# Fifteen of sixteen hidden pairs by seven products in an MLP's down projection, and an earlier place for the join of their sums on VectorE

## What is computed

```
h = rmsnorm(x, norm_mlp)
x = x + square(relu(h @ w_up)) @ w_down      # w_up 1024 x 4096, w_down 4096 x 1024
x = rmsnorm(x, norm_final)                   # end of the first block
proj = rmsnorm_2(x, norm_mix_2) @ w_in_2     # start of the second block
```

## Time and profile before

| | us |
|---|---|
| median of 3 runs | 952.59 |
| lowest, highest | 952.55, 954.3 |
| the profiled execution | 952.69 |
| its span on the core | 950.6 |
| PE busy in it | 942.7 (99%) |
| DVE busy | 706.8 (74%) |
| ACT busy | 561.2 (59%) |
| POOL busy | 129.9 (14%) |

### The profile page before, as it was taken

One profiled execution on the slowest core, in us unless ns is written; L12 is line 12 of the kernel. 1 busy time (PEld: TensorE's weight loads), 2 busy tenths in 40 slices (PEclk: granted clock), 3 DMA queues, 4 the chain that ended last, 5 costly groups with the idle time before them and its releaser, 6 DMA issues.

```text
span 950.6 us, 17020 instructions
## 1 busy us (share of the span) xinstructions
PE 942.7 (99%) x6900; PEld 868.9 (91%) x6900; DVE 706.8 (74%) x941; ACT 561.2 (59%) x856; POOL 129.9 (14%) x181
## 2 busy tenths in 40 slices
PE   9999999999999999999999999999999999999997
PEld 7877899989999999989988999998998899999996
DVE  5767875778877887878876787776666567777777
ACT  5677554557666666656865674545455445555544
POOL 2000001005223320414000001100000012121210
PEclk9999999999999999999999999999999999999999
DMA  9974447455666666556465365555645346565661
GB/s 302 310 244 126 121 128 179 160 177 176 200 192 192 194 194 199 174 172 199 139 194 163 105 204 173 174 183 174 198 159 174 115 156 205 173 202 176 202 197 67
DMA packets 133551, 170.45 MB, mean 179 GB/s; under 512 B 5824, under 2 KB 97296, under 8 KB 133472
## 3 DMA queue, kind: packets, MB, share of 16 engines
q1 hardware_dynamic: 131408, 165.07, 56.1%
q10 hardware_dynamic: 1424, 2.84, 0.9%
q0 software_dynamic: 640, 1.44, 0.7%
HBM read 168.28 MB, written 1.05 MB: 178 GB/s over the span
## 4 chain that ended last, share of the span: by engine, by line
PE 95%; DVE 2%; DMA 1%; ACT 1%; issue 1%; SPq 0%; POOL 0%; POOLq 0%; ACTq 0%; DVEq 0%
PE ps L442 24%; PE ps L409 15%; PE ps L410 15%; PE ps L413 15%; PE ps L391 4%; PE ps L524 3%; PE ps L859 3%; PE ps L863 3%; PE ps L858 3%; PE ps L803 2%; PE ps L799 2%; PE ps L800 2%; PE ps L556 1%; PE ps L559 1%; PE ps L555 1%; DMA raws<-in_w_in 1%
## 5 line engine op out<-in xcount | busy, mean ns | idle before, releaser
L1738 DVE TENSOR_TENSOR parts<-raws,parts 128x1024 fp32r<-128x1024 f32 (+3 forms) x307 | 364.4, 1202 | 125.4 <-ACT parts L1180 124.5
L1180 ACT ACTIVATE parts<-raws 128x1024 fp32r<-128x1024 f32 (+3 forms) x307 | 309.1, 1029 | 124.8 <-PE ps L413 50.4
L409 PE MATMUL ps<-room_r,parts 128*128 128x256 f32 x1248 | 308.6, 281 | 0.0
L410 PE MATMUL ps<-room_r,parts 128*128 128x256 f32 x1248 | 306.4, 279 | 0.0
L442 PE MATMUL ps<-parts,room_r 128*128 128x512 f32 (+1 forms) x1008 | 237.7, 392 | 0.4 <-ACT parts L1180 0.4
L409 PEld LDWEIGHTS ps<-room_r,parts 128*128 128x128 f32 x1248 | 234.3, 188 | 2.2 <-issue 0.8
L410 PEld LDWEIGHTS ps<-room_r,parts 128*128 128x128 f32 x1248 | 235.0, 188 | 1.2
L442 PEld LDWEIGHTS ps<-parts,room_r 128*128 128x128 f32 x1008 | 184.2, 188 | 42.9 <-issue 1.2
L413 PE MATMUL ps<-room_r,parts 128*128 128x256 f32 x1248 | 196.6, 279 | 0.0
L413 PEld LDWEIGHTS ps<-room_r,parts 128*128 128x128 f32 x1248 | 167.7, 188 | 0.0
L1772 DVE TENSOR_TENSOR room_r<-room,room_r 128x512 fp32r<-128x512 f32 (+2 forms) x74 | 52.5, 714 | 31.3 <-ACT room_r L1469 10.1
(11 more groups left out here) (245 smaller groups left out, 1133.4 us busy)
## 6 DMA issues: line engine op xcount, KB each, us to landing
raws<-in_w_in SPq DMA_DIRECT2D x99, 512.0 KB, 4.5
raws<-in_w_ffn_in SPq DMA_DIRECT2D x44, 512.0 KB, 4.6
raws<-in_w_up SPq DMA_DIRECT2D x32, 512.0 KB, 3.9
raws<-in_w_down SPq DMA_DIRECT2D x32, 512.0 KB, 3.7
raws<-in_w_ffn_out SPq DMA_DIRECT2D x22, 512.0 KB, 4.3
raws<-in_w_xkv SPq DMA_DIRECT2D x16, 512.0 KB, 4.3
raws<-in_w_out SPq DMA_DIRECT2D x8, 512.0 KB, 4.5
raws<-in_w_up_ssd SPq DMA_DIRECT2D x8, 512.0 KB, 4.6
```

The costliest lines, as they stand in the source:

```text
L409: e.matmul(ps, wh, hT[0][:, k, :], start=k == 0, stop=False)
L410: e.matmul(ps, wh, hT[1][:, k, :], start=False, stop=False)
L1180: e.activation(t.h, t.raw, ACT.Copy).then_inc(s["hi"], 1)
L1738: e.tensor_tensor(t.l, t.raw, t.h.bitcast(F32), ALU.subtract).then_inc(s["lo"], 1)
```

## The change

`by_sums[0]` grows from 14 to 15 pairs, so that `down(14, 0)` too is made by `down_by_sums`; only pair 15 is left to the 12 plain matmuls. The join's place in DVE's list was set by `until`, from when the last seven-product pair ends; for this MLP it is now set by a tile number: the join stands right behind the rest of B13. The other MLP keeps its rule.

```diff
-        by_sums = [range(14), range(1, 10)]
+        by_sums = [range(15), range(1, 10)]
...
-        where = {}
+        where, last_rest = {}, {}
...
                     if h:
                         where["down", u, q] = Group(None, count, None)
+                        last_rest[u, q] = w_.i
...
-                until(where["product", u, 1].at)
+                if u:
+                    until(where["product", u, 1].at)
+                else:
+                    while lo <= last_rest[u, 13]:
+                        rest_of_tile()
                 e.wait_ge(s["first_product"], u + 1)
```

## The result

The changed kernel takes 959.03 us (median of 6 runs, 958.76 to 960.5), the kernel before 952.62 us (6 runs, 952.18 to 954.3). The ratio is 1.0067, 95% interval 1.0057 to 1.0077: 6.4 us slower. The forecast was 956.7 us with a range to 958.4, so the kernel became slower as forecast, and the time lies 0.6 us above the range. The profiled execution took 959.11 us, its span is 957.2 us.

What follows compares the result with a forecast made beforehand. PE, busy 942.7 of 950.6 us, was taken as the bound, so each new wait is paid in full. -0.32 + 0.1 + 3.6 + 0.7 = +4.1 us gave 956.7 us, range 955.2 to 958.4.

Steps and rivals of the forecast that it cites:

- The matmuls, -0.32 us: On PE, pair 14 goes from 12 plain matmuls (2.80 us) to 21 (2.48 us): 0.32 us less.
- Pair 14's inputs are covered: In down(14, 0), S14 and the activation sums with their rests are ready before PE wants them: no wait.
- The join at 377.6, held by ACT's copy: On DVE, the join starts at 377.6 instead of 376.46, 1.1 us later, because ACT's copy ends only at 377.55.
- 0.1 us at the eight transposes: PE reaches the eight transposes at 381.48; the second add ends about 381.9, giving a stall of 0.1 us.
- The stall of 3.6 us: Before the four transposes: B14's later rest delays C2's load, ACT waits ahead of x, PE waits 3.6 us.
- 0.7 us in C2: PE waits 0.7 us after C2's first eight matmuls, as C2's rest stands behind x times norm_final; bounds 0 and 1.
- The clock: Rival: TensorE's clock falls in the 3.6 us stall, half speed costs 2 us, time 958.7 us; chance 0.06.

Runs made afterwards that it cites:

- the run with x ahead of C2: The changed kernel with ACT's rounding of the transposed x ahead of C1 and C2; 953.92 us, ratio 1.0013 to the kernel before.
- the run of 14 pairs reordered: Kernel before, with the join behind B13's rest and ACT's join copy, x's rounding and C2's rest on DVE moved earlier; 952.49 us, ratio 0.9999.

## Why the prediction was wrong, point by point

- **The matmuls, -0.32 us:** right. PE reaches the eight transposes when the sum says, once the start's 0.5 us are taken off.
- **Pair 14's inputs are covered:** right. The waits of PE name no product of pair 14.
- **The join at 377.6, held by ACT's copy:** right, 378.31 - 0.5 = 377.8, and DVE's idle time ahead of it (0.65 us) is ended by the copy.
- **0.1 us at the eight transposes:** too small. From their start to the next matmul it is 1.07 us (382.02 to 383.09), where it was 0.80 us (381.80 to 382.60); the second add ends only at 381.21 + 1.41 = 382.62. In the run with x ahead of C2 they take as long. The term is 0.3 us.
- **The stall of 3.6 us:** right in its chain and its size. PE is idle for 3.43 us; from the start of the last two matmuls ahead of it to the transposes it is 4.06 us (388.30 to 392.36) instead of 0.47 us (387.80 to 388.27 before), 3.6 us more. C2's load was forecast at 383.1 (383.78 - 0.5 = 383.3) and 3.7 us long (ACT starts 3.82 us behind it, 383.78 to 387.60), x at 387.9 (388.56 - 0.5 = 388.1), the end of the wait at 391.7 (392.36 - 0.5 = 391.9). The chain was cut at two places, the load's lateness and the order on ACT, and each cut took about 5 us away.
- **0.7 us in C2:** right. From 401.34 the next start should be 401.46 and is 402.15, 0.69 us.
- **The clock: the step that failed.** The sum put the fall of TensorE's clock at nothing; it stood among the rivals only, with the time 958.7 (959.03 measured), the price 2 us (1.67 measured) and a chance of 0.06, and the upper end of the range, 958.4, left it out. The chance came from the earlier trace rows, where the clock held for over 4 us of rest, so that a wait of 3.6 us seemed to fall short. That reading was wrong: those rows show **when** the clock changed in one execution, not how much rest it takes. Here the level changed about 4 us behind the last full matmul too (388.9 to 392.8), but a rest of 3.4 us was enough, and PE was already at work when the price came due. Nor is "over 4 us" steady: at the end of the program, where nothing of this was changed, the clock falls between 2.1 us (the run of 14 pairs reordered) and 5.2 us (the run with 5 matmuls of the identity) behind the last matmul. The windows of both, in this order:

```profile
944.00:945.00 1.00, 0.17 (x2) 0.00 (x0) 1.00 (x3) 0.61 (x1) 0.01 (x1) 1.00 0.00 0
...
946.00:947.00 1.00, 0.00 (x0) 0.00 (x0) 0.43 (x2) 0.38 (x1) 0.53 (x1) 0.62 0.89 344
```

```profile
948.00:949.00 1.00, 0.53 (x5) 0.32 (x3) 0.74 (x2) 0.72 (x1) 0.38 (x2) 1.00 0.00 0
...
953.00:954.00 1.00, 0.00 (x0) 0.00 (x0) 0.00 (x0) 0.00 (x0) 0.00 (x0) 0.85 0.94 365
```

A mean of 0.62 in the microsecond of 946 is a fall at 946.24, with the last matmul done at 944.17; 0.85 in that of 953 is a fall at 953.70, with the last done at 948.53. One row of an end could not say that 3.6 us was too short. "TensorE: Matmul & The Clock Gate", section "HAM oscillation — how this bites in real kernels" of the Trainium skill, describes this effect of a wait on a load: the work behind it starts at the lower clock. The trace agrees, with 3.43 us idle and 0.50 granted from 392.8 us on.

The sum with the measured terms is -0.3 + 0.3 + 3.6 + 0.7 + 1.7 = 6.0 us. In the two profiles the matmuls that want C2's rest come 6.47 us later (395.68 to 402.15), of which 0.49 us are the start's (14.52 to 15.01): 5.98 us. So the timelines leave nothing open up to there. The medians differ by 6.4 us; the 0.4 us that are left are as much as the wait at the program's start differs between executions, and stay open.

## What to carry to other kernels

On engines that go through fixed lists, moving a step also moves the release of a buffer, and with it a load; look for what stands behind that load's consumer on **its** engine, since that is where the delay grows. Where PE is busy 99% of the time, a saving of 0.3 us of matmuls is no reason to touch an order that is just covered: each uncovered wait is paid in full. And a forecast stall on TensorE as long as the one here (3.4 us) should be priced with the fall of its clock; the moment at which the clock fell at the end of one execution is no measure of how much rest it takes.

## What the runs showed of the hardware

In the traced execution a rest of PE of 3.43 us brought the clock to its lower level for about 3.4 us, beginning when PE was at work again, at a cost of 1.67 us. Waits of 1.42 us and 1.01 us did not. A rest of 2.08 us with 1.1 us of unused matmuls ahead of it did not in the traced execution, but in two of its four runs the mean clock (0.996 and 0.997) suggests a fall. At the end of the program the clock fell 2.1 to 5.2 us behind the last matmul. Filling the stall nearly whole with 14 unused matmuls kept the mean clock at 0.998 or 0.999 in all four runs and made this kernel 1.3 us faster than the changed one; 5 of them gave 0.9 to 2.3 us, from run to run.
